# The gated delta rule in chunks of 128 tokens in place of 64, with the state's first products left out

## What is computed

```python
gc = cumsum(g, within the chunk)
decay = exp(where(lower_incl, gc[..., :, None] - gc[..., None, :], -inf))
lmat = where(strict, (k * beta) @ k.T * decay, 0)
tinv = triangular_solve(eye + lmat, eye)
u = tinv @ (v * beta)
w = tinv @ (k * beta * exp(gc))
attn = (q @ k.T) * decay
def step(state, ...):
    v_new = u - w @ state
    o = (q * exp(gc)) @ state + attn @ v_new
    state = state * exp(g_last) + (k * exp(g_last - gc)).T @ v_new
    return state, o
```

## Time and profile before

| | us |
|---|---|
| time, median of 3 runs | 2384.91 |
| lowest and highest run | 2381.79, 2385.09 |
| the profiled execution's own time | 2385.34 |
| its span in the trace | 2384.0 |

### The profile page before, as it was taken

How to read it: one execution, slowest core, us unless ns; L and a number is a source line. 1 busy time by engine, 2 the same in 40 slices (tenths; PEclk the granted TensorE clock), 3 DMA queues, 4 the chain that set the end, 5 groups by cost and what they waited for, 6 DMA issues and landing times.

```text
span 2384.0 us, 27707 instructions
## 1 busy us (share of the span) xinstructions
PE 2340.0 (98%) x11308; PEld 1937.5 (81%) x11308; DVE 1381.1 (58%) x1978; ACT 1164.3 (49%) x1655; POOL 9.6 (0%) x17
## 2 busy tenths in 40 slices
PE   8999999999999999999999999999999999999997
PEld 6788788888788888888888887888888888888886
DVE  5676655656555676686655555655455444554454
ACT  5456654555654554453445445445444344434443
POOL 0000000000000000000000000000000000000000
PEclk9999999999999999999999999999999999999999
DMA  7454445554445542332444445555555555555552
GB/s 259 137 178 141 143 157 194 177 178 156 162 160 193 164 159 89 116 132 100 166 159 159 144 168 175 180 193 192 185 192 183 190 192 193 182 190 194 189 181 106
DMA packets 204271, 400.13 MB, mean 168 GB/s; under 512 B 12656, under 2 KB 12816, under 8 KB 203760
## 3 DMA queue, kind: packets, MB, share of 16 engines
q1 hardware_dynamic: 201920, 391.08, 48.6%
q0 software_dynamic: 1648, 6.32, 0.9%
q10 hardware_dynamic: 576, 0.95, 0.1%
HBM read 396.23 MB, written 2.10 MB: 167 GB/s over the span
## 4 chain that ended last, share of the span: by engine, by line
PE 92%; DVE 4%; ACT 2%; issue 1%; DMA 0%; DVEq 0%; ACTq 0%
PE ACC L797 27%; PE ACC L799 27%; PE ACC L798 27%; PE TP L429 2%; ACT arena L820 1%; DVE WL L1686 1%; PE PV L624 1%; PE SC L619 1%; PE SC L466 1%; PE TP L474 1%; PE SC L677 1%; PE PV L627 1%; PE PV L483 0%; PE PV L484 0%; PE PV L482 0%
## 5 line engine op out<-in xcount | busy, mean ns | idle before, releaser
L1686 DVE TENSOR_TENSOR WL<-W,WH 128x1024 fp32r<-128x1024 f32 x740 | 901.0, 1220 | 646.7 <-ACT WH L820 644.9
L820 ACT ACTIVATE WH<-W 128x1024 fp32r<-128x1024 f32 x740 | 781.3, 1056 | 846.8 <-PE ACC L799 844.0
L797 PE MATMUL ACC<-WH,XH 128*128 128x512 f32 x2592 | 1046.8, 404 | 7.0 <-ACT arena L820 4.8
L799 PE MATMUL ACC<-WH,XL 128*128 128x512 f32 x2592 | 1014.0, 391 | 0.0
L798 PE MATMUL ACC<-WL,XH 128*128 128x512 f32 x2592 | 1012.3, 391 | 0.0
L797 PEld LDWEIGHTS ACC<-WH,XH 128*128 128x128 f32 x2592 | 488.6, 188 | 117.0 <-issue 15.2
L799 PEld LDWEIGHTS ACC<-WH,XL 128*128 128x128 f32 x2592 | 487.7, 188 | 105.7
L798 PEld LDWEIGHTS ACC<-WL,XH 128*128 128x128 f32 x2592 | 489.2, 189 | 91.9 <-issue 1.0
L797 PE MATMUL ACC<-WH,HH 128*128 128x512 f32 x352 | 139.5, 396 | 0.0
L799 PE MATMUL ACC<-WH,HL 128*128 128x512 f32 x352 | 137.8, 392 | 0.0
L798 PE MATMUL ACC<-WL,HH 128*128 128x512 f32 x352 | 137.4, 390 | 0.0
(11 more groups left out here) (260 smaller groups left out, 1491.4 us busy)
## 6 DMA issues: line engine op xcount, KB each, us to landing
W<-in_w_in SPq DMA_DIRECT2D x84, 1024.0 KB, 4.8
W<-in_a_w_in SPq DMA_DIRECT2D x48, 1024.0 KB, 5.1
W<-in_w_ffn_gate SPq DMA_DIRECT2D x44, 1024.0 KB, 5.0
W<-in_w_ffn_up SPq DMA_DIRECT2D x44, 1024.0 KB, 5.0
W<-in_w_ffn_down SPq DMA_DIRECT2D x44, 1024.0 KB, 5.1
W<-in_b_w_in SPq DMA_DIRECT2D x40, 1024.0 KB, 5.0
W<-in_a_w_out SPq DMA_DIRECT2D x16, 1024.0 KB, 5.0
W<-in_b_w_out SPq DMA_DIRECT2D x16, 1024.0 KB, 5.1
```

Of the source, the lines that this page charges most:

```text
L797: MM(out, hx, WH[:, k, 0:ch.width], start=q == 0 and k == 0, stop=False)
L799: ins = MM(out, lx, WH[:, k, 0:ch.width], start=False, stop=last and k == QK - 1)
L820: return nc.scalar.activation(out, in_, func, **how)
L1686: TT(tiles_of(M.WL[n % 2], ch, half), tiles_of(M.W[n % 4], ch, half), tiles_of(M.WH[n % 2], ch, half).bitcast(F32), ALU.subtract).then_inc ...
```

## The change

The chunk becomes the whole block of 128 tokens. The masks no longer cut it in two, the inverse has one more level (LEVELS = 7, levels 1 to 6), and the loop over c is gone. For t = 0 the state is zero: the queries' scaling, the state reads and their products are left out, and the state after it is the sum alone, copied out of PSUM. For t = 1 the state is read by the plain keys (PE L618, beside the first level's transposes), scaled row by row and subtracted from the scaled values on DVE (L1498), and then one product with the inverse gives the new values up to their sign, which ACT puts right in its copy. No state is made behind t = 1, so its transposed keys are left out. L1500's multiply (now L1505) moves into level 2. A block has 18 steps.

```diff
@@ pe_program dn @@
             for h in range(PH):
-                TR(tp[:, h * P:(h + 1) * P], block(1, h), ident)
+                if t == 0:
+                    TR(tp[:, h * P:(h + 1) * P], block(1, h), ident)
                 ins = TR(tp[:, (PH + h) * P:(PH + h + 1) * P], block(2, h), ident)
...
             for h in range(PH):
                 ins = TR(sc[:, h * P:(h + 1) * P], m["M"][:, h, :], ident)
+            if t:
+                pe.wait_ge(*at("dn_state", i, s))
+                for h in range(PH):
+                    ins = MM(sc[:, (PH + h) * P:(PH + h + 1) * P], block(1, h), m["STATE"][:, h, :], start=True, stop=True)
             ins.then_inc(*did("dn_level_turned", i, s, t))
...
-                MM(sc[:, h * P:(h + 1) * P], m["S"][:, h, :], m["VB"][:, h, :], start=True, stop=True)
-                ins = MM(sc[:, (PH + h) * P:(PH + h + 1) * P], m["KBG"][:, h, :], m["S"][:, h, :], start=True, stop=True)
-            for c in range(P // DC):
...
+                ins = MM(sc[:, h * P:(h + 1) * P], m["S"][:, h, :], m["VB"][:, h, :], start=True, stop=True)
+            ins.then_inc(*did("dn_new_sums", i, s, t))
+            yield
+            pe.wait_ge(*at("dn_new_values", i, s, t))
+            for h in range(PH):
+                hs = slice(h * P, (h + 1) * P)
+                if t:
+                    MM(tp[:, hs], m["QD"][:, h, :], m["STATE"][:, h, :], start=True, stop=False)
+                ins = MM(tp[:, hs], m["DT"][:, h, :], m["VN"][:, h, :], start=t == 0, stop=True)
+            if t == 0:
+                for h in range(PH):
+                    ins = MM(pv[:, h * P:(h + 1) * P], m["KD"][:, h, :], m["VN"][:, h, :], start=True, stop=True)
@@ act_program dn @@
-            A(flat(m["EGR"]), sc[:, lo], ACT.Exp)
+            if t:
+                A(flat(m["EGR"]), sc[:, lo], ACT.Exp)
...
+            A(flat(m["VN"]), sc[:, lo], ACT.Copy, scale=-1.0 if t else 1.0).then_inc(*did("dn_new_values", i, s, t))
@@ dve_program dn @@
-            TT(m["KBG"], pairs(tp[:, lo]), per_head(of(BEG, t)), ALU.mult)
-            TT(m["KD"], pairs(tp[:, lo]), per_head(of(EKD, t)), ALU.mult)
+                TT(m["KD"], pairs(tp[:, lo]), per_head(of(EKD, t)), ALU.mult)
...
-            TT(m["DT"], pairs(tp[:, hi]), m["DT"], ALU.mult)
...
             TT(m["M"], m["L"], over_heads(masks[:, 1, :]), ALU.mult)
+            if t:
+                for h in range(PH):
+                    STT(m["VB"][:, h, :], sc[:, (PH + h) * P:(PH + h + 1) * P], of(BEG, t)[:, h:h + 1], m["VB"][:, h, :], ALU.mult, ALU.subtract)
             TT(m["S"], over_heads(M.ident), pairs(sc[:, lo]), ALU.subtract).then_inc(*did("dn_solved", i, s, t, 0))
...
+                if level == 2:
+                    TT(m["DT"], pairs(tp[:, hi]), m["DT"], ALU.mult)
...
+            if t == 0:
+                V.tensor_copy(m["STATE"], pairs(pv[:, lo])).then_inc(*did("dn_state", i, s))
```

More of the change, by code:

```diff
@@ L75, in more_constants @@
         levels.append((j // (2 * b) == i // (2 * b)) & (j % (2 * b) >= b) & (i % (2 * b) < b))
-    dn = [np.ones((P, P)), same & (j <= i), same, np.where(same & (i <= j), 0, NEG)] + levels
+    dn = [np.ones((P, P)), j <= i, np.where(i <= j, 0, NEG)] + levels
     q, c = np.arange(T), np.arange(PADC)
@@ L355, in memory @@
     at = 19456
-    for n, size in dict(ones=P, tri=P, same=P, lower=P, levels=LEVELS * P, conv=24 * 4, dt=DH, alog=DH).items():
+    for n, size in dict(ones=P, tri=P, lower=P, levels=LEVELS * P, conv=24 * 4, dt=DH, alog=DH).items():
         dn[n], at = cut(at, size), at + size
@@ L538, in dn_gates @@
         MM(TP[0][:, 0:TB * DH], M.dn["tri"], G, start=True, stop=True)
-        MM(TP[0][:, TB * DH:2 * TB * DH], M.dn["same"], G, start=True, stop=True).then_inc(*did("dn_summed"))
+        MM(TP[0][:, TB * DH:2 * TB * DH], M.dn["ones"], G, start=True, stop=True).then_inc(*did("dn_summed"))
         emptied["TP0"] = ("dn_sums_taken",)
@@ L654, in dn @@
+            yield
             emptied[TPn] = ("dn_outputs_taken", i, s, t)
-            emptied[SCn] = ("dn_new_values", i, s, t, 1)
-            emptied[PVn] = ("dn_state", i, s, t, 1)
+            emptied[SCn] = ("dn_new_values", i, s, t)
+            emptied[PVn] = ("dn_state", i, s) if t == 0 else ("dn_solved", i, s, t, LEVELS - 1)
     def compress_turn():
@@ L1017, in dn @@
                 yield
[L1018 to L1020 removed]
+            act.wait_ge(*at("dn_new_sums", i, s, t))
+            A(flat(m["VN"]), sc[:, lo], ACT.Copy, scale=-1.0 if t else 1.0).then_inc(*did("dn_new_values", i, s, t))
             yield
[L1022 to L1033 removed]
+            act.wait_ge(*at("dn_outputs", i, s, t))
+            col = i * CH + s * PH * HD
+            for h in range(PH):
+                ins = A(M.OD[:, t, col + h * HD:col + (h + 1) * HD], tp[:, h * P:(h + 1) * P], ACT.Copy, scale=M.dn_norms[:, s, h * TB + t:h * TB + t + 1])
+            ins.then_inc(*did("dn_outputs_taken", i, s, t))
+            yield
     def dn_out():
@@ L1521, in dn @@
             yield
-            for c in range(P // DC):
-                r = slice(c * DC, (c + 1) * DC)
-                dve.wait_ge(*at("dn_state_read", i, s, t, c))
-                other = slice((1 - c) * DC, (2 - c) * DC)
-                V.memset(m[f"VN{c}"][other], 0.0)
-                TT(m[f"VN{c}"][r], m["U"][r], pairs(sc[:, lo])[r], ALU.subtract).then_inc(*did("dn_new_values", i, s, t, c))
-                yield
-                end = c * DC + DC - 1
-                dve.wait_ge(*at("dn_outputs", i, s, t, c))
-                for h in range(PH):
-                    ins = STT(m["STATE"][:, h, :], m["STATE"][:, h, :], m["EGR"][:, h, end:end + 1], pv[:, h * P:(h + 1) * P], ALU.mult, ALU.add)
-                ins.then_inc(*did("dn_state", i, s, t, c))
-                yield
+            if t == 0:
+                dve.wait_ge(*at("dn_state_sums", i, s))
+                V.tensor_copy(m["STATE"], pairs(pv[:, lo])).then_inc(*did("dn_state", i, s))
+            yield
     def dn_out():
```

51 lines of the change are left out of this document (10 added, 41 removed).

## The result

| | us |
|---|---|
| before, median of 5 | 2384.74 (2381.79 to 2385.09) |
| after, median of 5 | 2364.33 (2363.75 to 2372.56) |
| ratio after to before | 0.9927, 95% interval 0.9912 to 0.9941 |
| profiled execution of after, its span | 2363.92, 2362.6 |
| predicted | 2365.4 (2361.0 to 2372.5) |

The kernel is 20.4 us faster by the medians, and 21.4 us by the spans of the two profiled executions. One thing in the table asks for an answer: two of the five executions of after took 2372.5 us, the other three 2363.8 to 2364.3.

What follows compares the result with a forecast made beforehand. TensorE was taken to bound the kernel, busy 98% of the span. 13.5 us less work plus 6.05 less waits made 19.5 us, taking the median from 2384.9 to 2365.4 us, range 2361 to 2372.5.

Steps and rivals of the forecast that it cites:

- PE is the bound, and its work is time: TensorE is busy 98% of the span; the delta-rule blocks lose 13.5 us of its work, all of it time.
- The waits are DVE's queue ahead of level 1: TensorE's waits for VectorE before the inverse's first product in the four blocks fall from 8.3 to 2.25 us.
- The dip at 903: Half clock in the first group's t = 0 block, costing 1.23 us on six main products, counted as gone.
- the 6.05: Microseconds of waits less ahead of the inverse's first product in the four blocks, 1.2 to 1.5 of it clock.
- "Some 49 us": Expected time from a group's first t = 0 transposes to those of t = 1, in place of 56.0 and 53.3.
- The compression "stays": The wait at 1182.78 for VectorE behind the output norm starts at a fixed visit and stays.
- rival 3: The 7 us half-clock dip behind the wait at 1182.78 is absent too: three more microseconds, 2362 us; chance 0.08.
- rival 1: The waits in the four blocks stay as they are, only the 13.5 us of work goes: 2371.4 us; chance 0.20.
- Rival 2: The clock falls more often: six dips in the blocks at 1.5 us give back 9 us, 2374 us; chance 0.08.
- Rivals 1, 4 and 5: 1: waits stay; 4: VectorE bounds block starts, above 2390 us, chance 0.02; 5: added steps cost what removed ones save.
- Rival 5: The extra inverse level and the state read cost as much as the removed steps: 2385 us; chance 0.02.

Runs made afterwards that it cites:

- version with the later compression: The kernel before with the first compression begun three visits later (5 to 8), nothing else: 2378.1 us, ratio 0.9975.
- the kernel with the scores put back: The changed kernel with VectorE's multiply of scores by decays put back ahead of level 1 instead of in level 2: 2365.5 us, ratio to before 0.9921.

## Why the prediction was right, and where it was not

- **PE is the bound, and its work is time.** Held: 120 records fewer, as counted. With products taken out of before (3.6 us for 3.6 counted) and put into after (3.5 for 3.6) the price per record was tested both ways.
- **The waits are DVE's queue ahead of level 1.** Held, size and place: 0.3, 0.8, 0.15 and 1.0 were laid out, 0.54, 0.84, 0.25 and 0.84 came, 2.5 for 2.25. The two new subtractions were taken as 0.55 us a pair and bounded by L1533; in after they show as 0.60 from start to end, with the next operation 0.52 behind the first:

```profile
946.88 0.60 DVE L1498 SCALAR_TENSOR_TENSOR arena<-SC,small_tables,arena 128x128 f32<-128x128 f32 x2
947.40 0.41 DVE L1499 TENSOR_TENSOR arena<-consts,SC 128x256 f32<-128x256 f32 x1
```

- **The dip at 903.** Counted as gone for good (1.2 of the 6.05). It is gone from after's traces, but the kernel before does not always have it either, as its version with the later compression shows. It was no sure gain; the term was for one execution.
- **"Some 49 us" from the first transposes of t0 to those of t1.** Wrong: 47.7 in the first group (890.25 to 937.98), 47.4 in the second (1039.71 to 1087.13). I took the work and the waits off 56.0 and 53.3 wrongly for a visit: an 18-step block in place of a 19-step one also has one visit of main products less in it, 1.36 us, which are done later and saved nobody anything. 56.0 - 3.6 - 3.2 - 1.4 is 47.8. The sum for the kernel was not touched by it.
- **The compression "stays".** Half right, and the step that mattered most for a reader of single times. The wait stayed (2.08 and 1.96). That the half clock behind it would stay at its 7 us was the unsaid part, and rival 3 had only its absence. It lasted 3.4 us in after's first profile in place of 6.8, which is worth 1.7 of the 1.9 us between the forecast sum (19.5) and the 21.4 of the spans, and 20.5 in the second. The median of five (2364.3) is the height with the short stretch; with six more executions the median of the changed kernel is 2369.6, still within the range, and its height is a matter of how many long ones are drawn. The range held both, for the reason of rival 1 (2371.4) and not for the right one; that part of it was luck.
- **Rival 2**, the clock falls more often, named the right resource at the wrong place. In the four blocks of after it never fell. Behind the compression it stayed low longer in 6 of 11 executions, by their times, which the ones of before did in 8 of the 55 beside the experiments (2390 us and over); and its price per case, 8 us, was about what I gave for six dips. Its reason, products taken out beside waits, is not shown: by the times, the kernel with the scores put back had no long stretch in six executions, and the one with the multiply moved in before had it in half of twelve, with no product taken out.
- **Rivals 1, 4 and 5** fell with the traces: the waits did not stay, DVE is busy for 137 of 203 us in the blocks, and the change does what it says. Rival 5's number was also wrong by its own terms: 13.5 us eaten up would leave the 6.05 of waits, so 2379 us and not 2385.

**Left open**: what beside the wait brings the half clock on, what makes the stretch end after 3.4, 6.8, 10.2 or 20 to 24 us, and why some kernels draw the long one often and others hardly ever. The instructions and the wait are the same in both traces of the changed kernel.

## What to carry to other kernels

Before a median is read, look whether the executions of a kernel stand at several heights, and take a profile of each height: here a gain of 4.3 us in the trace showed as a ratio of 1.000, and one number in an order table, one visit, was worth 4 us at one height and 12 at the other. The wait of 2 us of TensorE ahead of the compression was not priced at 2 us: starting the products one visit later gave back 4 to 12. Where a stretch at half clock follows a wait, try to take away what it waits for, or start the products later. And when blocks are compared start to start, take out of the difference the main work that merely sits in another block.

## What the runs showed of the hardware that I had not expected

TensorE's clock stayed at its lower level for 20.5 to 23.9 us while the engine was busy in every microsecond of it (20.50 of 20.50, at a granted clock of 0.51), with products of 30 columns, transposes and groups of six main products in turn. The same products, one to three visits later, ran at 1.00 when no 2 us wait stood ahead of them. So whether the engine is busy by its records does not tell at which level it will be. The Trainium skill, page "TensorE: Matmul & The Clock Gate", Part 1 ("The two states you'll see"), has the full rate come back once the array is kept busy; these stretches do not agree with that as far as "busy" is what a profile's busy column shows. What it has ahead of the fall, idling, fits in kind only: a wait of 1.96 us or more stands ahead of each of these stretches, but the one of 2.51 us at 617 has none behind it in any trace.
